# Matrix products that visit the columns of x in eight different orders

## The reference, cut to what matters

```
# first block, two layers
h = h + 0.5 * swiglu_ffn(rms_norm(h, ...), ffn1_w_in, ffn1_w_out)      # 1024 -> 2 x 2816 -> 1024
h = h + hybrid_mixer(rms_norm(h, ...), w_in, ..., w_out)
h = h + memory_cross_attention(rms_norm(h, ...), rms_norm(mem, ...), w_q, w_kv, w_o)
h = h + 0.5 * swiglu_ffn(rms_norm(h, ...), ffn2_w_in, ffn2_w_out)
# second block, two layers
z = rms_norm_2(h, norm_g) @ w_in
...
h = h + jnp.concatenate([oa, ob], axis=-1) @ w_out
gate = jax.nn.sigmoid(rms_norm_2(h, ple_norm_g) @ w_ple_gate)
return h + (p_i @ w_ple) * gate
```

## Time and profile before

| | us |
|---|---|
| two timed runs | 3067.81 and 3070.95, median 3069.38 |
| profiled execution, its own time | 3071.06 |
| its span, first to last instruction | 3069.1 |
| PE busy | 3038.4 (99%) |
| PEld, DVE, ACT, POOL busy | 2604.3, 1994.1, 1497.6, 150.1 |
| lines 346 and 3371 on the chain that ended last | 60% and 22% of the span |

### The profile page before, as it was taken

How to read it: one execution, slowest core, us unless ns; L and a number is a source line. 1 busy time by engine, 2 the same in 40 slices (tenths; PEclk the granted TensorE clock), 3 DMA queues, 4 the chain that set the end, 5 groups by cost and what they waited for, 6 DMA issues and landing times.

```text
span 3069.1 us, 45374 instructions
## 1 busy us (share of the span) xinstructions
PE 3038.4 (99%) x19194; PEld 2604.3 (85%) x19194; DVE 1994.1 (65%) x2741; ACT 1497.6 (49%) x2083; POOL 150.1 (5%) x158
## 2 busy tenths in 40 slices
PE   9999999999999999999999999999999999999999
PEld 8999887888788998989887788789998886888777
DVE  8677549854584866758447855576675568554774
ACT  5444436553453544435335653454444558454673
POOL 0000000300000000000000300000000006000150
PEclk9999999999999999999999999999999999999999
DMA  4233221132122323232221122122322220222202
GB/s 160 97 115 107 107 83 59 39 124 83 69 97 91 122 86 112 90 112 102 98 85 67 56 86 108 55 97 98 110 98 100 94 83 29 81 104 83 83 31 88
DMA packets 49545, 275.29 MB, mean 90 GB/s; under 512 B 5312, under 2 KB 8896, under 8 KB 26304
## 3 DMA queue, kind: packets, MB, share of 16 engines
q1 hardware_dynamic: 49344, 272.40, 25.2%
HBM read 270.28 MB, written 2.10 MB: 89 GB/s over the span
## 4 chain that ended last, share of the span: by engine, by line
PE 91%; DVE 5%; ACT 2%; issue 1%; DMA 0%; SPq 0%; POOL 0%; DVEq 0%; ACTq 0%; POOLq 0%
PE banks L346 60%; PE banks L3371 22%; PE banks L2618 1%; PE banks L2659 1%; ACT weights L2999 1%; DVE weights L3047 1%; PE banks L1688 1%; PE banks L1838 1%; PE banks L1654 0%; PE banks L1674 0%; ACT slab_hi L314 0%; DVE weights_turned L3068 0%; PE banks L1851 0%; PE banks L3790 0%; PE banks L1709 0%
## 5 line engine op out<-in xcount | busy, mean ns | idle before, releaser
L346 PE MATMUL banks<-x_hi,slab_hi 128*128 128x512 f32 x1488 | 588.5, 396 | 0.7 <-DVE dil_v L892 0.5
L346 PE MATMUL banks<-x_hi,slab_lo 128*128 128x512 f32 x1488 | 579.5, 389 | 0.0
L346 PE MATMUL banks<-x_lo,slab_hi 128*128 128x512 f32 x1488 | 579.4, 389 | 0.0
L314 ACT ACTIVATE slab_hi<-slab_raw 128x2048 fp32r<-128x2048 f32 (+2 forms) x207 | 351.0, 1696 | 467.0 <-PE banks L346 446.5
L321 DVE TENSOR_TENSOR slab_lo<-slab_raw,slab_hi 128x2048 fp32r<-128x2048 f32 (+2 forms) x203 | 409.7, 2018 | 172.4 <-ACT slab_hi L314 172.2
L3371 PE MATMUL banks<-x_blocks_hi,x_area_parts 128*128 128x256 f32 x1736 | 398.9, 280 | 0.0
L346 PE MATMUL banks<-hidden_parts,slab_hi 128*128 128x512 f32 x1280 | 394.2, 389 | 0.0
L346 PEld LDWEIGHTS banks<-x_hi,slab_hi 128*128 128x128 f32 x1488 | 279.4, 188 | 65.9 <-issue 9.2
L346 PEld LDWEIGHTS banks<-x_lo,slab_hi 128*128 128x128 f32 x1488 | 279.5, 188 | 59.5 <-issue 2.9
L346 PEld LDWEIGHTS banks<-x_hi,slab_lo 128*128 128x128 f32 x1488 | 279.3, 188 | 58.7
L3371 PE MATMUL banks<-x_blocks_hi,slab_lo 128*128 128x256 f32 x1072 | 299.1, 279 | 0.0
(11 more groups left out here) (458 smaller groups left out, 5568.9 us busy)
## 6 DMA issues: line engine op xcount, KB each, us to landing
slab_raw<-slabs SPq DMA_DIRECT2D x195, 1024.0 KB, 4.8
slab_raw<-slabs SPq DMA_DIRECT2D x64, 704.0 KB, 4.0
slab_raw<-slabs SPq DMA_DIRECT2D x16, 640.0 KB, 3.8
h<-xT SPq DMA_DIRECT2D x8, 256.0 KB, 5.8
memory<-memT SPq DMA_DIRECT2D x2, 1024.0 KB, 5.3
out<-h SPq DMA_DIRECT2D x7, 256.0 KB, 4.8
constants<-con SPq DMA_DIRECT2D x1, 1284.5 KB, 9.9
slab_raw<-slabs SPq DMA_DIRECT2D x4, 256.0 KB, 5.2
```

The source lines that it names most:

```text
L314: self.nc.scalar.activation(self.wh[:, g % self.HIGHS, 0:w], self.raw[:, g % self.RAWS, 0:w], ACT.Copy).then_inc(self.hi_ready, 1)
L346: mm = self.nc.tensor.matmul(out, left[a], right[c], start=start and n == 0, stop=stop and n == 2)
```

## The change

The new function `walked(a, walk)` returns a view of the same columns in another order; `walk` 0 is the normal one. `products` and `tensor_unit` apply the same view to the streamed operand (both its high and low part) and to the output in PSUM, so that column t of x still lands in column t of the bank. Only the time order of columns within one matmul differs. `pair` and `tensor_plain` pass the chunk number i, so chunk 0 is straight and chunks 1 to 7 use walks 1 to 7. `tensor_unit` passes 2n, so its four blocks use walks 0, 2, 4 and 6. The calls in `tokens`, `wide`, `deep` and `gate` leave `walk` at 0.

For 512 columns the walks are: 1, pairs of columns that alternate between the two halves; 2, the same backwards; 3, pairs that alternate among four quarters; 4, runs of 16 that alternate between halves; 5, pairs 16 columns apart, that is every eighth pair, in eight sweeps; 6, the same backwards; 7, every sixteenth pair, in sixteen sweeps. The pairs start at even columns.

```diff
--- before.py
+++ after.py
@@ -152,6 +152,24 @@
         else:
             runs.append([n, n + 1])
     return runs
+
+
+def walked(a, walk):
+    if walk == 1:
+        return a.rearrange("p (h j e) -> p j h e", h=2, e=2)
+    if walk == 2:
+        return a[:, ::-1].rearrange("p (h j e) -> p j h e", h=2, e=2)
+    if walk == 3:
+        return a.rearrange("p (h j e) -> p j h e", h=4, e=2)
+    if walk == 4:
+        return a.rearrange("p (h j e) -> p j h e", h=2, e=16)
+    if walk == 5:
+        return a.rearrange("p (j h e) -> p h j e", h=8, e=2)
+    if walk == 6:
+        return a[:, ::-1].rearrange("p (j h e) -> p h j e", h=8, e=2)
+    if walk == 7:
+        return a.rearrange("p (j h e) -> p h j e", h=16, e=2)
+    return a
 
 
 class Kernel:
@@ -340,8 +358,8 @@
         return tuple(a.rearrange("p (s k c) -> p k s c", s=2, k=KC // 2)[:, i]
                      for a in (self.wh[:, g % self.HIGHS, :], self.wl[:, g % self.RAWS, :]))
 
-    def products(self, out, left, right, start, stop):
-
+    def products(self, out, left, right, start, stop, walk=0):
+        out, right = walked(out, walk), [walked(a, walk) for a in right]
         for n, (a, c) in enumerate(((0, 0), (0, 1), (1, 0))):
             mm = self.nc.tensor.matmul(out, left[a], right[c], start=start and n == 0, stop=stop and n == 2)
         return mm
@@ -738,7 +756,7 @@
         outs = [k.ps[:, job.bank, 0:cols] for job in self.jobs[s]]
 
         def product(c, i):
-            return k.products(outs[c], w((i * 2 + c) * P), (xh[:, i, 0:cols], xl[:, i, 0:cols]), i == 0, i == KC - 1)
+            return k.products(outs[c], w((i * 2 + c) * P), (xh[:, i, 0:cols], xl[:, i, 0:cols]), i == 0, i == KC - 1, i)
         if fresh:
 
             for i in range(KC):
@@ -3343,7 +3361,7 @@
             pe.wait_ge(k.split_done, slab.g + 1)
 
         def product(c, i):
-            return k.products(k.ps[:, slab.jobs[c].bank, :], w((i * 2 + c) * P), (xh[:, i, :], xl[:, i, :]), i == 0, i == KC - 1)
+            return k.products(k.ps[:, slab.jobs[c].bank, :], w((i * 2 + c) * P), (xh[:, i, :], xl[:, i, :]), i == 0, i == KC - 1, i)
         if s == 0:
             for i in range(KC):
                 if early:
@@ -3366,9 +3384,9 @@
 
     def tensor_unit(self, s, u, out, start):
         for n in range(self.BLOCK):
-            left, right = self.parts(s, u, n), (self.bh[:, u, n, :], self.bl[:, u, n, :])
+            left, right = self.parts(s, u, n), [walked(b[:, u, n, :], 2 * n) for b in (self.bh, self.bl)]
             for a, c in ((0, 0), (0, 1), (1, 0)):
-                mm = self.k.nc.tensor.matmul(out, left[a], right[c], start=start and n + a + c == 0,
+                mm = self.k.nc.tensor.matmul(walked(out, 2 * n), left[a], right[c], start=start and n + a + c == 0,
                                              stop=n == self.BLOCK - 1 and a == 1, skip_group_check=True)
         return mm
```

## The result

The changed kernel takes 3845.53 us (two runs, 3845.30 and 3845.76) against 3069.38 us: a ratio of 1.2521, with a 95% interval of 1.2501 to 1.2542. It is 776 us slower. I had forecast no change, 3070 us, with a range up to 3550 us.

The account below looks back on a forecast made before the run. PE, busy 99% of the span, was taken to bound the kernel, each matmul distance paid in full. Profiled 3071.06 us plus 0 for stepped patterns gave 3071 us, 3070 us as timed; range 3040 to 3550 us.

Parts of the forecast that it names:

- What bounds the kernel: Whole kernel: PE is busy 99% of the span, so time is the sum of distances between matmuls; other engines have slack.
- The price of a stepped pattern: Stepped matmuls in projections and block products: what a stepped order adds to one matmul, taken as zero on 1280 us exposed.
- My bound from below: Small fp32 products at line 1851 read runs of 2 columns at 29.0 ns against 28.1 straight: no price seen.
- The bound from above: Unrounded fp32 products take two cycles a column; that rate would add 202 ns per 512 columns, 98 ns per block product.
- The two rules of the Trainium skill: On PSUM: one says any non-contiguous pattern slows matmuls significantly; the other asks only that every two consecutive elements be contiguous.
- Every jump is paid: Rival, chance 0.14: all stepped patterns fall to two cycles a column, adding 1108 us, so 4180 us.
- Backward walks: Rival, chance 0.10: only walks 2 and 6, running downwards through memory, fall to two cycles a column, so 3545 us.
- A wait between chunks: Rival, chance 0.04: at each change of order PE waits for the last columns to land, 0.162 us each, so 3490 us.
- A part of it: Rival, chance 0.04: only the long steps (walks 5 to 7) or a cycle per jump in some cost, 3100 to 3400 us.
- The remainder goes away: Rival, chance 0.06: stepped matmuls lose the 12 and 10 ns beyond their column cycles, 85 us less, 2985 us.
- the 12 ns: Rounded matmuls of 512 columns: what 226.8 ns leaves beyond 214.5 ns at one column a cycle.

## Why the prediction was wrong

**What bounds the kernel** was right. PE's distances are paid in full: the distances of three kinds of matmul, and of the straight ones between them, account for the whole 774 us of longer span, with the other engines busy as long as before, and the two parts of the change add within 3 us.

**The price of a stepped pattern** is the step that failed. I took zero and it was 142.5 ns on a matmul of 512 columns in the mean over all eight chunks, and 38.9 ns on a block product. The reason I gave, that walks keep aligned pairs, names the wrong unit for the reading side: x is read in aligned lines of 16 bytes, four columns each (runs of 4 take 243 ns on a line's start and 437 ns across two lines). The rate that fits the runs is at best one new line in four cycles of the 2.4 GHz clock, 1.67 ns. At one column a cycle, a straight read needs exactly that. A pair uses half a line, so 256 pairs need 256 x 4 cycles = 427 ns, and walks 5 and 6 showed 430 and 433. That lines are the unit and that reading pays is shown; why two places in turn are cheaper than this rate, and some patterns dearer, is not.

**My bound from below** was misread. The earlier trace rows show pairs without a price, but at two cycles a column, where there is time for a whole line per pair, as the unrounded pairs at 429 ns confirmed. I had called this bound loose and then leaned on it as the nearest row. It was nearest in shape and not in rate. The bound from above, two cycles a column, turned out close to the truth for half of the walks (3, 5, 6, 7: 430 to 470 ns against my 429), for a reason that I did not have.

**The two rules of the Trainium skill** that I weighed were both about the bank, and on the bank neither price appeared: a stepped write cost nothing in pairs (ratio 0.9998) or in single columns at half the pace. The Trainium skill, PSUM — Partial Sum Buffer, section Specifications (TRN2), says that any non-contiguous pattern slows matmuls significantly. No write here did, and the measurement decides. What bears on the reading side I had not weighed: the Trainium skill, SBUF — State Buffer, section Specifications (TRN2), gives lines of 16 bytes and asks for at least two hits in each for full bandwidth. The line is confirmed here; two hits were enough at 429 ns for 512 columns and not at 227, where four were needed.

**The rivals.** *Every jump is paid* (0.14, 4180 us) was nearest in mechanism, wrong in the memory it came with, and too dear: walks 1 and 2 cost about 110 and 120 ns instead of 202, walk 4 only 20, and block products with runs of 16 only 7 (125 ns). *Backward walks* (0.10) fell: walk 6 costs what walk 5 does, walk 2 only 10 to 15 ns more than walk 1, and whole backward reads take 231 to 240 ns. *A wait between chunks* (0.04) is not there: writes with changing orders alone left every distance at 227 ns. *A part of it* (0.04) had the right idea, that walks differ, but the wrong list and size. *The remainder goes away* (0.06) was no gain for the kernel, yet its mechanism is partly real: with one or two lines read again and again, a matmul takes some 215 ns and not 227, which suggests that the 12 ns belong to fetching lines; no run shows it for an order that visits all columns.

**The range** was set from one mechanism a case. With the price unknown between 0 and 1108 us, and bounds so far apart, 0.62 on one end was too much, and the upper end should have stayed near the full price.

## What to carry to other kernels

Cost an access pattern by the side it is on and by bytes per unit of time, not by its number of jumps: count how often the streamed operand goes to a new aligned line of 16 bytes, and compare 4 cycles for each with the cycles its columns need. This is an estimate. It was within 11% for the pairs of walks 3, 5, 6 and 7, too dear for two places in turn (427 ns against 328), and too cheap for some patterns below. For rounded fp32 keep runs of 4 columns or more that start on a line; for the output, order was free in everything tried. And a row that shows no price bounds only patterns at its own rate.

## What the runs showed of the hardware that I had not expected

- The order of writes into a PSUM bank was free in all that was tried: 227 ns for 512 columns in all eight orders of the change, six of them in pairs, and single columns at 429 ns.
- Lines are kept for a moment: two lines read in turn again and again cost 217 ns, four 563 ns; two places that each use a line twice cost 321 to 343 ns, at distances from 32 to 2048 bytes.
- Some patterns cost more than one line in four cycles: 493 ns for two places 2 KB apart and 563 ns for four places 512 bytes apart, where 427 would be expected, and 490 to 555 ns for every 32nd pair. What collides there is open.
- Stepped reads also slow their neighbours a little: a straight chunk between them takes 237 ns in place of 227, and the weight loads of these products show 197 in place of 188 ns.
- A weight load runs beside every matmul here, and no run separates the two reads. It is unlikely to set the rate of lines: beside an unrounded matmul of 920 ns it lasts 187 to 210 ns, about a fifth of the time, and a line still took 1.80 ns there.
